# Two groups of SBUF buffers change places in a hand-placed transformer kernel

## The reference, cut to what matters

```python
def reference(x, ...):
    x = first_block(x, ...)      # rmsnorm; z = h @ w_in; gates = sigmoid(h @ w_gate + b_gate)
                                 # gMLP, pooling and differential attention mixers, gated and summed
                                 # x += merged @ w_out;  x += conv_ffn(rmsnorm(x), w_up, conv_w, conv_b, w_down)
    return second_block(x, ...)  # rms_norm; block attention and gated linear attention; x += [o_a, o_g] @ w_out
                                 # cross attention on mem (256 tokens); x += relu(h @ w_up)**2 @ w_down; rms_norm
```

## Time and profile before

| what | value |
|---|---|
| median of 3 runs | 1473.87 us (1473.71 to 1474.26) |
| the profiled execution's own time | 1474.26 us |
| its span, first to last instruction | 1472.5 us |
| mean granted TensorE clock | 0.997 |
| TensorE matmul busy | 1460.1 us, 99% |
| TensorE weight loads busy | 1206.5 us, 82% |
| VectorE busy | 965.7 us, 66% |
| ScalarE busy | 624.9 us, 42% |
| GpSimd busy | 24.8 us, 2% |
| mean transfer rate | 102 GB/s |

### The profile page before, as it was taken

How to read it: one execution, slowest core, us unless ns; L and a number is a source line. 1 busy time by engine, 2 the same in 40 slices (tenths; PEclk the granted TensorE clock), 3 DMA queues, 4 the chain that set the end, 5 groups by cost and what they waited for, 6 DMA issues and landing times.

```text
span 1472.5 us, 19778 instructions
## 1 busy us (share of the span) xinstructions
PE 1460.1 (99%) x7108; PEld 1206.5 (82%) x7108; DVE 965.7 (66%) x1504; ACT 624.9 (42%) x898; POOL 24.8 (2%) x22
## 2 busy tenths in 40 slices
PE   9999999999999999999999999999999999999997
PEld 7878888888888888888888888788888888888886
DVE  6837774676655556434357887957656685868677
ACT  5214554324433333333234555525444544435353
POOL 0000000000000000000000000000000000000000
PEclk9999999999999999999999999999999999999998
DMA  6623222223322322233332333213204333140401
GB/s 231 237 86 100 78 78 86 86 87 114 93 93 99 100 98 89 100 113 101 129 96 91 114 97 119 76 60 124 74 30 173 128 126 104 55 162 14 171 0 58
DMA packets 40564, 149.79 MB, mean 102 GB/s; under 512 B 4360, under 2 KB 4872, under 8 KB 38324
## 3 DMA queue, kind: packets, MB, share of 16 engines
q1 hardware_dynamic: 36384, 138.95, 27.9%
q10 hardware_dynamic: 4116, 9.96, 2.0%
HBM read 146.76 MB, written 6.06 MB: 104 GB/s over the span
## 4 chain that ended last, share of the span: by engine, by line
PE 98%; DMA 0%; ACT 0%; issue 0%; DVE 0%; POOL 0%; SPq 0%; POOLq 0%; ACTq 0%
PE ps L1238 31%; PE ps L1239 31%; PE ps L1240 31%; PE ps L1389 1%; PE ps L1402 1%; PE ps L2518 1%; PE ps L1279 0%; DMA tables<-tables_dram 0%; PE ps L1272 0%; PE ps L2538 0%; PE ps L2678 0%; PE ps L2550 0%; PE ps L1447 0%; PE ps L2618 0%; ACT mix L1820 0%
## 5 line engine op out<-in xcount | busy, mean ns | idle before, releaser
L1238 PE MATMUL ps<-hh,wh 128*128 128x512 f32 x1088 | 430.8, 396 | 0.0
L1240 PE MATMUL ps<-hh,wl 128*128 128x512 f32 x1088 | 424.0, 390 | 0.0
L1239 PE MATMUL ps<-hl,wh 128*128 128x512 f32 x1088 | 423.8, 390 | 0.0
L604 ACT ACTIVATE wh<-stage 128x1024 fp32r<-128x1024 f32 x194 | 205.4, 1059 | 373.5 <-PE ps L1240 369.3
L835 DVE TENSOR_TENSOR wl<-stage,wh 128x1024 fp32r<-128x1024 f32 x193 | 235.9, 1223 | 113.1 <-ACT wh L604 112.7
L1238 PEld LDWEIGHTS ps<-hh,wh 128*128 128x128 f32 x1088 | 204.4, 188 | 46.4 <-issue 4.3
L1240 PEld LDWEIGHTS ps<-hh,wl 128*128 128x128 f32 x1088 | 204.3, 188 | 43.2
L1239 PEld LDWEIGHTS ps<-hl,wh 128*128 128x128 f32 x1088 | 204.6, 188 | 39.4
L1761 ACT ACTIVATE wh<-raw 128x1024 fp32r<-128x1024 f32 x56 | 59.4, 1061 | 73.5 <-PE ps L1240 73.4
L1238 PE MATMUL ps<-wh,xch 128*128 128x512 f32 x224 | 87.1, 389 | 0.0
L1239 PE MATMUL ps<-wl,xch 128*128 128x512 f32 x224 | 87.1, 389 | 0.0
(11 more groups left out here) (358 smaller groups left out, 2316.2 us busy)
## 6 DMA issues: line engine op xcount, KB each, us to landing
stage<-stream_dram SPq DMA_DIRECT2D x222, 512.0 KB, 3.5
raw<-down_dram SPq DMA_DIRECT2D x16, 1024.0 KB, 6.2
bias_lines<-bias_line ACTq DMA_DIRECT2D x1, 3840.0 KB
bias<-bias_lines ACTq DMA_DIRECT2D x4, 512.0 KB, 5.0
out_dram<-scaled SPq DMA_DIRECT2D x4, 512.0 KB, 2.6
x<-x_dram SPq DMA_DIRECT2D x3, 512.0 KB, 7.6
bias<-bias_lines ACTq DMA_DIRECT2D x4, 256.0 KB, 3.0
mem<-mem_dram ACTq DMA_DIRECT2D x1, 1024.0 KB, 4.9
```

The source lines that it names most:

```text
L604: A(parts_of(b, p)[0], b.stage[:, p.slot, :], ACT.Copy).then_inc(s.hi_ready, 1)
L1238: MM(out, wh, xh, start=start, stop=False, skip_group_check=True)
L1239: MM(out, wh, xl, start=False, stop=False, skip_group_check=True)
L1240: return MM(out, wl, xh, start=False, stop=stop, skip_group_check=True)
```

## The change

Only byte offsets change. The persistent group starts at 0 instead of 112 KB. The region starts behind it, at `r0`, instead of at 0. The absolute offsets of the six overlaid tensors change from 128 KB to 16 KB. Sizes, the order of buffers in each group, instructions, loops, semaphores and transfers are the same.

```diff
@@ def place(nc)
-    off = [112 * KB]
+    off = [0]
...
     b.turn = nxt("turn", [8])
     b.small2 = nxt("small2", [64])
-    R = lambda kb: kb * KB
+    r0 = off[0]
+    R = lambda kb: r0 + kb * KB
...
-    b.gsq = at("gsq", 128 * KB, [4, T])
-    parts = 128 * KB
+    b.gsq = at("gsq", 16 * KB, [4, T])
+    parts = 16 * KB
     b.ke = at("ke", parts, [2, 2 * T])
     b.ee = at("ee", parts + 8 * KB, [2, 2 * T])
```

## The result

| | before | changed |
|---|---|---|
| median of 5 runs | 1473.71 us (1473.34 to 1474.26) | 1481.56 us (1481.37 to 1482.91) |
| ratio | 1 | 1.0054, 95% interval 1.0044 to 1.0065 |
| profiled execution, span | 1472.5 us | 1479.4 us |

The forecast was 1473.9 us with a range of 1472.2 to 1475.6. The measured 1481.56 lies outside it. The loss of 7.85 us is five times the interval's half-width (0.00105 x 1473.7 = 1.5 us).

A forecast was written before the change was run, and what follows sets the result against it. The prediction took TensorE's own matmul pace as the bound. The profiled 1474.26 us plus 0 each for TensorE, other engines and transfers gave 1474.26, or 1473.9 us as a median, range 1472.2 to 1475.6.

The forecast's parts named there:

- What bounds the kernel: Whole span: TensorE busy 99%, at its own pace of 0.680 us a triple, with waits of 2.6 us in all.
- How far the buffers move: Persistent group down 114688 bytes, region up 113280; modulo 256 the group keeps its phase, the region flips by 128.
- TensorE: Matmul operand reads: no new kind of arrangement, so 0 us, kept within 1.3 us either way.
- The four arrangements: Matmul operands both persistent, both in the region, or one in each either way; means 389 to 390 ns before the change.
- The bound of 1.3 us: TensorE's range either way: 0.084% of 1460 us of matmul time gives 1.2 us, kept as 1.3.
- The slower rival: Panel pipeline: writes by ScalarE, VectorE or transfers hold up TensorE's reads; 0.42 ns a matmul or more; chance 0.04.
- VectorE, ScalarE and transfers: Work beside TensorE, head and tail: 0 us, with 0.3 us either way kept for transfers.
- The estimate of 0.15 us on the last store: Last store of 2.6 us: a 128-byte flip makes transfers about 6% cheaper or dearer by transaction count, 0.15 us.
- The signs to look for: Changed profile: `ah` stretch 119.0 us, `xch` stretch 282.2; growth of 0.3 us or more in either means slower TensorE.

The follow-up runs named there:

- m1: Separate kernel, only TensorE working on zeros: 23 sections of 128 fp32r matmuls with different operand starts; 226.8 ns a matmul at difference 0, 232.3 at 128.
- e3: Kernel before with the persistent group starting 128 bytes later: 1481.56 us, ratio 1.0054.
- e8: Changed kernel with the region starting 128 bytes later: 1473.86 us, ratio 1.0002.
- e7: Kernel before with 128 bytes of small vectors moved in front of `stage` and 128 behind; TensorE's operand pairs keep multiples of 256: 1474.11 us, ratio 1.0001.
- e2: Kernel before with the 14976 bytes from `rrow` on placed between the region and `x` to `wl`: 1482.33 us, ratio 1.0055.
- e5: Kernel before with a gap of 128 bytes between `hl` and `stage`: 1499.86 us, ratio 1.0178.
- e1: Kernel before with `x` to `wl` at 0 to 96 KB, the region behind them, the vectors from `rrow` on last: 1473.95 us, ratio 1.0001.
- e4: Kernel before with the persistent group 256 bytes later, `small2` moved in front of it: 1474.01 us, ratio 1.0001.

## Why the prediction was wrong

**What bounds the kernel** held: TensorE at its own pitch, waits of 2.8 us. It is also why so small an effect counted in full.

**How far the buffers move** was right to the byte, and "modulo 256 the persistent group keeps it and the region flips by 128" is the very cause. It was put to use for the transfers alone.

**TensorE** is the step that failed: "The change makes no new kind of arrangement [...] I take 0 us." The four arrangements of the earlier trace rows differed in group and in absolute offset, but in all of them the starts of the two buffers differed by a multiple of 1 KB. Equal pitch over all of them says nothing about a distance that none of them had. The bound of 1.3 us was the precision of that comparison and no bound of an unknown cost. In its place the runs showed a cost of 5.5 to 6.6 ns for each product of 512 columns that pairs the groups. For `xch` that is 3 x 224 x 5.5 ns = 3.7 us, measured 3.8. For `ah`, `parts_of` puts the weights of 103 triples into `wh`, and of the other 73 into `wh4`, which stands in the region. Two stretches of the changed kernel, one of each kind, with the matmuls that read `ah`:

```profile
602.00:630.00 28.00, 25.16 (x82) 15.01 (x80) 0.69 (x1) 0.63 (x1) 1.00 0.29 95
633.00:641.50 8.50, 7.66 (x26) 4.79 (x26) 0.00 (x0) 0.00 (x0) 1.00 0.21 67
```

Before the change they held 84 and 26. From the starts, the matmuls of the first stretch follow each other by 233.3 ns and those of the second by 226.7, so 103 triples x 3 x 6.6 ns = 2.0 us, measured 2.1. That these lose 6.6 ns, and the same 128 bytes 5.5 ns with `xch` and in m1, is not explained. The remaining 7.8 - 5.9 = 1.9 us is in the smaller pairs; `yabh` by `wh` went from 389 to 392 ns, for example. A gap of 128 bytes alone made all of it (e3), 128 bytes of padding took it away (e8), and TensorE alone shows it (m1).

**The slower rival** had the right place in the numbers, "1 ns would give 1473.9 + 7.1 = 1481 us", for a wrong reason. It named writers that disturb reads and expected a hit on the panel pipeline; that pair was spared, m1 has no writers, and e7 moves the writers' buffer at no cost. Its 1 ns is a mean (7.85 us / 7108 = 1.1 ns) of nothing for most matmuls and of 5 ns and more for those across the groups. The reason given against it, that each group keeps its own distances, left out the pairs across the groups.

**VectorE, ScalarE and transfers** at nothing: right. Line 836 is at 1223 ns as before, `raw` lands in 6.4 us (expected within 0.4 of 6.2), the stores in 2.6, and the tail from `y` on takes 15.1 us, as forecast. The estimate of 0.15 us on the last store was drawn from the Trainium skill, "DMA: Bandwidth & Descriptors" (How a descriptor splits into AXI transactions). It counted transactions; by the beats that the same section counts it would be an estimated half of that. The trace's 2.6 us is the same at both phases, so it shows no such cost, at a precision of 0.1 us. The landing of `raw` can't test it: in e2 and e3, with the region at its old place, it is 7.0 and 6.9 us.

**The signs to look for** did their work. The two distances of 119.0 and 282.2 us grew by 2.1 and 3.8 us, where 0.3 had been named as the point from which TensorE's pace had changed.

## What to carry to other kernels

Where TensorE runs fp32r products of 512 columns back to back, start every buffer that it reads, moving or weights, at the same place modulo 256 bytes, and at a multiple of 32. Rounding each group's start up to 256 does both and costs at most 255 bytes of a partition. The mismatch cost 0.5% here, and 1.8% in e5. A row of small vectors of 32-byte sizes in front of the large buffers is enough to lose it. And before an effect is called zero because places do not matter, ask which remainders the rows have in common: a comparison bounds only what varies in it.

## What the runs showed that was not expected

- TensorE's pitch at 128x128 by 512 in fp32r is 226.8 ns when the starts of the operands differ by 0, 256, 512, 1024 or 1536 bytes, and 228.3 to 233.9 ns at the others tried, with no other engine at work. The Trainium skill, in "SBUF — State Buffer" (Who interferes with whom), gives TensorE two read ports, one for the moving operand and one for weight loads, and calls them independent; these rows show that the place of one operand against the other changes the pace, and the measurement decides.
- The loss does not grow with the difference: 32, 64, 96, 160 and 224 bytes cost 6 to 7 ns, 128 bytes 5.5, and 192 bytes 1.5. So it depends on direction at 64 bytes (64 on: 233.9, 64 back, which is 192: 228.3) and not at 32 (233.1 both ways). It vanishes where the matmul is narrower (256 columns) or its operands are bf16 or plain float32. Why is not shown.
- Both operands at 4 bytes take (456.1 - 425.7) / 127 = 239.4 ns though their difference is 0, both at 16 bytes (425.5 - 395.9) / 127 = 233.1; both at 32 bytes (365.7 - 337.0) / 127 = 226.0 and at 64 and 128 bytes 226.8, the same within the 0.8 ns. Of the starts tried, those that are no multiple of 32 bytes cost by themselves.
- The layouts without such differences (before, e1, e4, e7, e8) all lie between 1473.7 and 1474.1 us. None is faster than the kernel before.
